# A three-part f32 network on one Trainium2 core: norm factors applied behind the first two weight blocks of each stage

## The reference

```python
def rmsnorm(x, g):
    xf = x.astype(jnp.float32)
    y = xf * lax.rsqrt(jnp.mean(xf * xf, axis=-1, keepdims=True) + RMS_EPS)
    return (y * g.astype(jnp.float32)).astype(x.dtype)
# N1, N2:          h + mixer(rmsnorm(h, g) @ w_in ...)
# N3:              x = rmsnorm(h, final_norm_g)[:, N_META:]; L0.n1 is a norm of this x
# L.n1, L.n2:      proj = rms_norm(x, norm1_g) @ w_in;  u = rms_norm(x, norm2_g) @ w_up
# C.n1, C.n2:      the same in the third block, ahead of w_in and of gate and up
# NQ, NKV:         norms of the 384 and 256 latent columns, ahead of w_uq and w_ukv
```

## Time and profile before

| | us |
|---|---|
| median of three runs | 2246.89 (2245.2 to 2249.37) |
| profiled execution, span | 2244.8 |
| TensorE busy | 2208.6 |
| TensorE weight loads busy | 1888.1 |
| VectorE busy | 770.7 |
| ScalarE busy | 411.9 |
| norms: sums ending near | 25, 217, 334 and 344, 787, 1024, 1466, 1702, 2004 |

### The profile page before, as it was taken

The page is one execution under the profiler, slowest core; times in us unless marked ns, Lnnn a source line. Parts: engine busy times, 40 slices in busy tenths (PEclk is TensorE's granted clock), DMA queues, the critical chain, the costliest instruction groups (busy, mean ns, idle before and its releaser), DMA issues.

```text
span 2244.8 us, 29477 instructions
## 1 busy us (share of the span) xinstructions
PE 2208.6 (98%) x10248; PEld 1888.1 (84%) x10248; DVE 770.7 (34%) x2196; ACT 411.9 (18%) x950; POOL 0.4 (0%) x7
## 2 busy tenths in 40 slices
PE   8999999999999999999999999999999999999998
PEld 6757878888888888888888888888888888888887
DVE  2142331791443145401692444145500023311100
ACT  2231221121112022200211112022201113211100
POOL 0000000000000000000000000000000000000000
PEclk9998998999999999999999999999999999999999
DMA  4312342433333434444433333444443432334443
GB/s 154 124 47 75 116 147 96 154 130 131 127 136 120 143 131 151 152 151 137 158 123 127 132 131 132 135 142 154 149 148 133 144 120 92 132 132 149 149 151 131
DMA packets 42160, 296.62 MB, mean 132 GB/s; under 512 B 4688, under 2 KB 4816, under 8 KB 8416
## 3 DMA queue, kind: packets, MB, share of 16 engines
q1 hardware_dynamic: 42080, 295.55, 38.5%
HBM read 294.48 MB, written 1.05 MB: 132 GB/s over the span
## 4 chain that ended last, share of the span: by engine, by line
PE 97%; DVE 1%; DMA 1%; ACT 1%; issue 1%; SPq 0%; DVEq 0%; ACTq 0%
PE bank L575 96%; PE bank L574 1%; DMA ring<-wstream 1%; DMA arena<-x 0%; DVE xn L1317 0%; DVE arena L1317 0%; ACT small L1028 0%; DVE arena L1632 0%; DVE arena L1625 0%; DVE small L1325 0%; ACT arena L1008 0%; DVE tmp L1628 0%; ACT arena L1121 0%; DVE tmp L1329 0%; ACT arena L1072 0%
## 5 line engine op out<-in xcount | busy, mean ns | idle before, releaser
L575 PE MATMUL bank<-xn,ring 128*128 128x256 f32 (+2 forms) x5760 | 1276.8, 385 | 5.9 <-DVE xn L1317 5.4
L575 PEld LDWEIGHTS bank<-xn,ring 128*128 128x128 f32 (+1 forms) x5760 | 1103.7, 192 | 174.1 <-issue 11.0
L575 PE MATMUL bank<-arena,ring 128*128 128x256 f32 (+2 forms) x2824 | 627.4, 383 | 4.8 <-DMA ring<-wstream 2.9
L575 PEld LDWEIGHTS bank<-arena,ring 128*128 128x128 f32 x2824 | 535.4, 190 | 86.9 <-issue 4.5
L1008 ACT ACTIVATE arena<-bank 128x256 f32 (+5 forms) x408 | 161.1, 397 | 1150.1 <-PE bank L575 976.5
L1317 DVE SCALAR_TENSOR_TENSOR arena<-arena,par (+1 forms) x712 | 299.9, 480 | 26.4 <-DVE arena L1317 3.7
L1317 DVE SCALAR_TENSOR_TENSOR arena<-arena,bank 128x256 f32<-128x256 f32 (+3 forms) x86 | 35.4, 423 | 253.9 <-ACT arena L1008 238.5
L1317 DVE SCALAR_TENSOR_TENSOR x_res<-bank,x_res 128x256 f32<-128x256 f32 x48 | 20.4, 425 | 289.2 <-PE bank L575 289.2
L575 PE MATMUL bank<-arena 128*128 128x256 f32 (+9 forms) x448 | 94.7, 349 | 0.9 <-ACT arena L1008 0.9
L1008 ACT ACT_TABLE_LOAD x53 | 68.0, 1283 | 132.5 <-PE bank L575 131.3
L575 PEld LDWEIGHTS bank<-arena 128*128 128x128 f32 (+5 forms) x448 | 62.5, 181 | 25.5 <-issue 15.9
(11 more groups left out here) (147 smaller groups left out, 690.6 us busy)
## 6 DMA issues: line engine op xcount, KB each, us to landing
ring<-wstream SPq DMA_DIRECT2D x262, 1024.0 KB, 4.8
ring<-wstream SPq DMA_DIRECT2D x15, 768.0 KB, 4.2
cst<-consts SPq DMA_DIRECT2D x1, 2616.0 KB, 15.8
ring<-wstream SPq DMA_DIRECT2D x4, 512.0 KB, 3.8
out<-arena SPq DMA_DIRECT2D x1, 1024.0 KB, 4.1
ring<-wstream SPq DMA_DIRECT2D x2, 384.0 KB, 3.2
ring<-wstream SPq DMA_DIRECT2D x2, 288.0 KB, 2.7
par<-params SPq DMA_DIRECT2D x1, 545.5 KB, 6.0
```

Source lines behind the costliest of these rows:

```text
L575: return pe.matmul(o, lhs, rhs, start=start, stop=stop, skip_group_check=True)
```

## The change

Nine norms of the residual stream (N1, N2, N3 with L0.n1, L0.n2, L1.n1, L1.n2, C.n1, C.n2) and the two of the latents are computed otherwise:

- `boundary`: ScalarE writes, behind each residual add, xg = x * gain (into free parts of the arena) and the square.
- `unscaled`: the next stage's first block, and then its second, take xg as operand, so they wait for no factor. The stages are split for this in the stream plan (B.u0, L.a0, L.up0, C.mqk0, C.up0); order and sizes of the weight stream stay as they were.
- GpSimd adds the squares of tiles 0 to 5 into one (`gather`), and TensorE, behind the first block, sums over the partitions with an all-ones 128 x 128 tile: three products (`stream_total`) that leave each token's sum on every partition. ScalarE takes the root of the whole 128 x T tile, VectorE inverts it (`invert`). There is no diagonal and no spread.
- VectorE empties the four tiles of the two blocks with a multiplication by the factor (`scaled`) and writes xn = xg * factor in between, for the third block on.
- N3 and L0.n1 are joined: xg is h * final gain * next gain, both sums run side by side on GpSimd, and L0.n1's factor is computed from both (eps is carried along). x_res gets its own factor later.
- The host lays the tokens out feature-major; SP loads them in two halves straight into h_res, the first ahead of the first weight block, the second behind it, with the constants' first part; the parameters are loaded in two parts, the larger behind A.lat1. The transposes go. N1's squares are ScalarE's. In A, NQ and NKV are inverted and latn is written ahead of the gate, in front of the small tables on VectorE.
- What followed from loops over all blocks is written out for the first two: their evictions, tanh, convolution and products (up0: `ffp0`, `conv0`, `ft0`, `hf0`; ScalarE waits for `hf0` before the loop).

```diff
-            def to_stream(stage, key, product, T):
-                for q in range(4):
-                    product(q)
-                    if q == 0 and key:
-                        banks = sum_banks(key, T)
-                    for j in range(2 * q - 2, 2 * q) if key and q else ():
-                        pe.wait_ge(*e.at((stage, "sq", j)))
-                        token_sums(key, banks, j, T, j == 0, False)
...
-                    norm_spread(key, T)
+            def total(key, T, terms):
+                b = e.take("side", (key, "sum"))
+                pe.wait_ge(*e.emptied((key, "sum")))
+                for n, (event, square) in enumerate(terms):
+                    pe.wait_ge(*e.at(event))
+                    ins = mm(b, slice(0, P), slice(0, T), C("ones"), square, n == 0, n == len(terms) - 1)
+                ins.then_inc(*e.side_done((key, "sum")))
+            def stream_total(key, T, squares):
+                total(key, T, [((key, "acc"), squares[:, 0, 0:T])] +
+                      [((key, "sq", j), squares[:, j, 0:T]) for j in (ND - 2, ND - 1)])
+            def unscaled(stage, keys, xg, T):
+                for q in range(2):
+                    halves(stage, q, 8, [P, P], lambda k: xg[:, k, 0:T], T,
+                           ready=None if q else [(keys[-1], "xg", j) for j in range(ND)])
+                    if q == 0:
+                        for key in keys:
+                            stream_total(key, T, sq_f if key == "L0.n1" else sq)
...
+            halves("A.lat0", 0, 8, [P, P], raw, TA, ready=[("N1", "xg", j) for j in range(ND)])
             pe.wait_ge(tables_in, 16)
...
+            stream_total("N1", TA, sq)
+            halves("A.lat1", 0, 8, [P, P], raw, TA)
+            halves("A.lat2", 0, 8, [P, ROPE], raw, TA)
+            total("NQ", TA, [(("NQ", "sq", j), sq[:, j, :]) for j in range(3)])
+            total("NKV", TA, [(("NKV", "sq", j), sq[:, 3 + j, :]) for j in range(2)])
+            blocks("A.gate", 8, xk(TA), TA, ready=normed("N1"))
...
+            def boundary(stage, key, buf, gain, xg):
                 act.activation(small[:, 58:59], small[:, 62:63], ACT.Sqrt).then_inc(*e.step())
                 for j in range(ND):
                     act.wait_ge(*e.at((stage, "x", j)))
+                    act.activation(xg[:, j, 0:buf.shape[2]], buf[:, j, :], ACT.Copy,
+                                   scale=G(gain, j)).then_inc(*e.step((key, "xg", j)))
+                    act.activation(sq[:, j, 0:buf.shape[2]], buf[:, j, :], ACT.Square).then_inc(*e.step((key, "sq", j)))
...
+            def gather(key, T, squares):
+                acc = squares[:, 0, 0:T]
+                pool.wait_ge(*e.at((key, "sq", 0)))
+                for j in range(1, ND - 2):
+                    pool.wait_ge(*e.at((key, "sq", j)))
+                    event = (key, "acc") if j == ND - 3 else (key, "part", j)
+                    pool.tensor_tensor(out=acc, in0=acc, in1=squares[:, j, 0:T], op=ALU.add).then_inc(*e.step(event))
+                    pool.wait_ge(*e.at(event))
...
+            def invert(key, T=S):
+                dve.wait_ge(*e.at((key, "rms")))
+                dve.reciprocal(inverse(key, T), inverse(key, T)).then_inc(*e.step((key, "inv")))
+                dve.wait_ge(*e.at((key, "inv")))
+            def scaled(key, norm, dst, rows=P, T=S, event=None, free=True):
+                dve.wait_ge(*e.at(("pe", key)))
+                b = e.bank_of(key)
+                dve.tensor_tensor(dst, psum[b][0:rows, 0:T], inverse(norm, T)[0:rows], ALU.mult).then_inc(*e.frees(key, event))
+            def normed(key, xg, T=S):
+                for j in range(ND):
+                    dve.tensor_tensor(xn[:, j, 0:T], xg[:, j, 0:T], inverse(key, T), ALU.mult).then_inc(*e.step((key, "xn", j)))
...
-                inverse_diagonals(L + "n2", S)
-                norm(L + "n2", ND, g("norm2_g_2"), lambda j: x_res[:, j, :], lambda j: xn[:, j, 0:S], S)
...
+                invert(L + "n2")
+                for t in range(2):
+                    scaled((L + "up0", 0, t), L + "n2", ffp[:, t, 2:S + 2], event=(L + "ffp0", 0, t))
+                normed(L + "n2", xg_f)
+                for t in range(2):
+                    scaled((L + "up0", 1, t), L + "n2", ffp[:, 2 + t, 2:S + 2], event=(L + "ffp0", 1, t))
```

More of the change, by code:

```diff
@@ L109, in stream_plan @@
     pl("C.o", "w_o_3", 0, 2, 2, 8, seq(0))
-    add("C.up", "w_ffn_gate_3+w_ffn_up_3", 0, its=11, n=2, size=2048,
-        part=lambda w, it, q: columns(w[q], span(256 * it)))
+    add("C.up0", "w_ffn_gate_3+w_ffn_up_3", 0, its=1, n=2, size=2048,
+        part=lambda w, it, q: columns(w[q], span(0)))
+    add("C.up", "w_ffn_gate_3+w_ffn_up_3", 0, its=10, n=2, size=2048,
+        part=lambda w, it, q: columns(w[q], span(256 * it + 256)))
     add("C.down", "w_ffn_down_3", 0, its=2, n=6, size=None, part=down_part)
@@ L836, in _ @@
             output1(MLA_H - 1)
-            out_product("A.out", "N2", lambda k: y1[:, k, :], TA, ready=[("y1", h) for h in range(MLA_H)])
+            out_product("A.out", lambda k: y1[:, k, :], TA, ready=[("y1", h) for h in range(MLA_H)])
+            unscaled("B.u0", ["N2"], xg_b, TA)
             blocks("B.u", 8, xk(TA), TA, ready=normed("N2"))
@@ L842, in _ @@
             blocks("B.g1", 8, xk(TA), TA)
-            out_product("B.out", "N3", lambda k: yb[:, k, :], TA, ready=[("yb", j) for j in range(ND)])
+            out_product("B.out", lambda k: yb[:, k, :], TA, ready=[("yb", j) for j in range(ND)])
             x256 = xk(S)
@@ L1147, in heads @@
                         out(h - 1)
-            def norm_squares(key):
-                for j in range(ND):
-                    square(sq[:, j, 0:S], x_res[:, j, :], (key, "sq", j), ("N3", "xn", j))
             def centred_squares(key, n, of, first=0):
@@ L1290, in _ @@
             heads("C.", probs3, probt3, 64 ** -0.5, moba_out, gates3, retention_part)
-            residual_squares("C.o", x_res)
-            token_root("C.n2", D, S)
-            with e.turns("C.up", 11) as i:
+            boundary("C.o", "C.n2", x_res, "norm2_w_3", xg_c)
+            rms("C.n2", D)
+            for t in range(2):
+                act.wait_ge(*e.at(("C.fo0", t)))
+                act.activation(ft3[:, t, :], fo3[:, t, :], ACT.Tanh, scale=0.5).then_inc(*e.step(("C.ft0", t)))
+            act.wait_ge(*e.at(("C.hf0",)))
+            with e.turns("C.up", 10) as i:
                 for t in range(2):
@@ L1897, in _ @@
             residual("C.o", x_res, S)
-            inverse_diagonals("C.n2", S)
-            norm("C.n2", ND, "norm2_w_3", lambda j: x_res[:, j, :], lambda j: xn[:, j, 0:S], S)
-            with e.turns("C.up", 11) as i:
+            invert("C.n2")
+            for t in range(2):
+                scaled(("C.up0", 0, t), "C.n2", fo3[:, t, :], event=("C.fo0", t))
+            normed("C.n2", xg_c)
+            for t in range(2):
+                scaled(("C.up0", 1, t), "C.n2", hf3[:, t, :], event=("C.u0", t))
+            for t in range(2):
+                dve.wait_ge(*e.at(("C.ft0", t)))
+                stt(fo3[:, t, :], ft3[:, t, :], 1.0, fo3[:, t, :], ALU.add, ALU.mult).then_inc(*e.step(("C.fg0", t)))
+            for t in range(2):
+                dve.wait_ge(*e.at(("C.fg0", t)))
+                dve.wait_ge(*e.at(("C.u0", t)))
+                dve.tensor_tensor(hf3[:, t, :], fo3[:, t, :], hf3[:, t, :], ALU.mult).then_inc(*e.step(("C.hf0",)))
+            dve.wait_ge(*e.at(("C.hf0",)))
+            with e.turns("C.up", 10) as i:
                 for t in range(2):
```

390 lines of the change are left out of this document (206 added, 184 removed).

## The result

| | us |
|---|---|
| kernel after, median of 4 runs | 2160.1 (2159.79 to 2166.84) |
| kernel before, beside it, median of 4 runs | 2248.13 (2245.2 to 2250.08) |
| ratio | 0.9618, 95% interval 0.9603 to 0.9633 |
| span of the profiled execution | 2158.4 (before 2244.8) |
| mean granted clock of TensorE | 0.996 (before 0.984) |

The forecast was 2163 us, 2.9 above what was measured. Of 2244.8 us of span, 86.4 went; the sum had said 84.0.

A forecast was written before the change was run, and what follows sets the result against it. TensorE's own stream was taken as the bound, with half-clock stretches behind norms hidden in its busy time. Terms 32.4 + 9.6 + 18.3 + 23.7 = 84.0 us took the 2244.8 us span to 2160.8, median forecast 2163 us, range 2152 to 2180.

The forecast's parts named there:

- Rival C: Whole kernel: matmul busy time is the truth and only idle time can go, about 2220 us; chance 0.03.
- The five norms (32.4): L0.n2, L1.n1, L1.n2, C.n1, C.n2: 38.9 us of norm cost less 6.5 of all-ones products, 32.4 us saved.
- N2 (9.6): Norm N2, at 272 columns: window and earlier sums go, less the all-ones products, 9.6 us saved.
- N3 with L0.n1 (18.3): Two norms in a row, joined: windows and sums go, less six all-ones products, 18.3 us saved.
- The norm's new timeline: Per norm, from t0, the last product tile's end: no TensorE wait remains; first xn near t0 + 12, wanted at 15.1.
- The start (23.7): Kernel start to first gate tile: 41.3 us against 63.2, plus 1.8 us of latent-norm spreads, 23.7 us saved.
- The gate's tight place: Start: VectorE must reach the gate loop near 30; TensorE wants the first gate bank 1.6 us later.
- GpSimd at no cost: GpSimd's adds of squares cost TensorE nothing; five may take 5.2 us each, the double norm's ten 2.9 each.
- Rival E: GpSimd's adds gate each total; at 6.7 us an add the gain is gone, at 7 about 2258 us; chance 0.02.
- A (clock keeps falling): At the norms the clock falls though the waits go, taking back 22 us: 2185 us; chance 0.09.
- B (VectorE late): VectorE late at gate and two up0: 2 us each plus some 2 us of half clock, 2175 us; chance 0.12.
- D (start gains nothing): First-block weights land late behind the tokens, so the start's 23.7 us are lost: 2187 us; chance 0.04.

The follow-up runs named there:

- experiment 2: Kernel after, but at the seven norms behind N1 TensorE waits for the first xn tile ahead of the second unscaled block: 2203.2 us, ratio 0.9802.
- experiment 3: Kernel after, but at the seven norms behind N1 TensorE waits only for ScalarE's root ahead of the second unscaled block: 2169.18 us, ratio 0.9653.
- Experiment 6: Kernel after with seven more same-size adds into a spare row ahead of each of GpSimd's 45: 2225.23 us, ratio 0.9899.
- experiment 8: Kernel after with dummy products on TensorE: seven before the first weights 2164.22 us, two at block A's attention wait 2156.92, both 2154.64; unchanged control 2159.87.

## Why the prediction was right, point by point

- **Reading by the granted clock and not by busy time: right.** Idle time fell by 14 us (36.2 to 21.9), the span by 86. Rival C would have ended at 2220.
- **The five norms (32.4), N2 (9.6), N3 with L0.n1 (18.3): right** to 0.4 us a stretch in the ladder, but for C.n1 to C.n2, where the trace of before held 1.5 us of lower clock outside any window. The window method works since it counts the lower clock wherever it lies between two marks.
- **The norm's new timeline: right.** xg at t0 + 1.17 (1.15), total at + 6.9, first xn at + 11.8 (12), third block at + 15.1. hf0 was there at t0 + 23.4 and not 26.1, since VectorE's steps take 0.41 to 0.50 us with hardly a hand-over where they don't wait for ScalarE; slack 4.8 us, not 2.4.
- **The start (23.7): 1.2 us short.** First product 7.82 (8.5), lat0 until 17.62, so 9.8 us (10.8), the rest 22.5 us (22.1). The half-clock stretch is the mis-sized term: (9.8 - 7.34) x 2 = 4.9 us at the lower level, not 7. The 7 us were those of N2 and L0.n2, the two long ones; the same reckoning gives 3.3 to 3.6 us for the four other windows of the earlier trace rows. So a choice among the rows made the error, and why it is 4.9 here no run shows. The gate's tight place held: the "near 30" of the text is no time of the kernel but can only count from N1's total, and VectorE multiplied at 49.4, 1.2 us before TensorE wanted the bank (1.6). The first eviction, forecast near 13 us, came at 23.0: VectorE can empty a bank only when it has the factor, which the sign left out. It cost nothing, since four banks were free. And the first latent tile of before ran 6.0 of its products at the lower pace, not 6.2 (6.44 us less 3.67, over 0.459 each); no term uses it.
- **GpSimd at no cost: right, and only the fact was missing.** An add of 128x256 takes 0.72 us, one of 128x272 0.78; VectorE's TENSOR_TENSOR of 128x256 takes 0.42, and in a row they follow each other by 0.35. Taking VectorE's row as the nearest was 0.3 to 0.37 us too low, which changed nothing; the prediction's estimate of 0.8 was nearer. Rival E's structure held at N3 and L0.n1, nearly at three of the norms, and at N2 once its tiles are counted at 3.67 us, but it missed N1, the earliest to break, and gave L1.n1 and C.n1 a limit that they don't reach.
- **A (clock keeps falling): refuted** by the rows at 1.00. **B (VectorE late): refuted**, though its price of 2 us of lower clock behind a wait was right for the long waits of experiment 2 (2.3) and wrong for short ones (experiment 3). **D (start gains nothing): refuted**, 24.9 us came of it (40.1 against 63.2, and the spreads' 1.8).
- **Instructions of TensorE: wrong, 9860 and not 9844.** I had counted two instructions for each of 16 transposes of full tiles in the 48; the timeline of before (7.72 to 16.9 us) has one for each of these and two for each of the eight small ones, so 32 go. It bore on no time.
- GpSimd shares its SBUF interfaces with VectorE, and the two contend where VectorE's instruction has two inputs in SBUF, says the Trainium skill (GPSIMD Engine Reference, section 8). Experiment 6 is no test of quite that, but of its neighbour: with eight times the adds, VectorE's residual adds, one input from PSUM and one from SBUF, take 425 ns as in the kernel after.

## What to carry over

Where an engine that is always busy sets the time, take its price from windows between two marks, each at the same point of the work, and let the granted clock say what is lost in them; of the 86 us only 14 were idle time. A factor that is the same for a whole token can follow the product, and two blocks of product cover a chain of sum, root, reciprocal and scaling of 5 us; a side engine may be slow at it, if each place where its result is wanted has its own limit reckoned, the first in the program above all. Here a wait of 0.56 us in a dense stream of products cost 0.8 us in all, and one of 3.5 us cost 5.5 or more.

## What the runs showed of the hardware

- TensorE's clock fell in four ways: behind single waits of 2.05 us (L0.n2 in experiment 6) and 3.5 us (experiment 2), behind 1.18 us among short products (block A's attention), behind or within one wait of 0.8 us that followed sums of one column (before: L0.n2, N2, N3; at the four others during the second wait or within 1 us behind it), and with no wait at all, from 450 to 475 us, where 20 instructions over only 16 partitions run ahead of the fall. It did not fall behind single waits of 0.5 to 0.6 us, of 1.4 us at L0.n1 (both experiment 3) or of 1.5 us at N2 in experiment 6, in dense streams of products.
- Products whose result nobody reads raise it and hold it (7.60 for 9.96 us; 1.00 for 0.66).
- In two single executions the mean clock was lower than in the others of the same kernel, 0.980 for 0.995 to 0.996 (2207.6 us for 2180) and 0.981 for 0.992 to 0.995 (2186 for 2164); in the first, which has a trace, it lay low for some 70 us on end.
- At the start the column shows 1.00 although the first block's pace is that of the lower level (9.96 us for 32 instructions that take 7.60 in experiment 8).
- GpSimd adding a tile to itself into another buffer takes 0.61 us, where the running sum in place takes 0.72.
